# Rotary embedding of the attention queries and keys taken from PSUM by the vector engine, in place of a permutation matmul

## The reference, cut to what matters

```python
def rms_norm(x, g):
    y = xf * lax.rsqrt(jnp.mean(xf * xf, axis=-1, keepdims=True) + EPS)
    return y * g
def rope(x, pos):                      # hd = 128
    ang = pos[:, None] * inv[None, :]
    cos, sin = jnp.cos(ang), jnp.sin(ang)
    x1, x2 = xf[..., :hd // 2], xf[..., hd // 2:]
    return concatenate([x1 * cos - x2 * sin, x2 * cos + x1 * sin], axis=-1)

mq = rope(rms_norm(split_heads(mq, 8), moba_q_norm_g), pos)
mk = rope(rms_norm(split_heads(mk, 8), moba_k_norm_g), pos)
```

## Time and profile before

| | |
|---|---|
| Median of 3 runs | 1398.55 us |
| The profiled execution's own time | 1399.14 us |
| Its span | 1397.3 us |
| TensorE matmul busy | 1188.5 us (85%) |
| VectorE busy | 840.2 us (60%) |
| ScalarE busy | 466.0 us (33%) |
| GpSimd busy | 533.9 us (38%) |
| Mean granted TensorE clock | 0.955 |

### The profile page before, as it was taken

The page is one execution under the profiler, slowest core; times in us unless marked ns, Lnnn a source line. Parts: engine busy times, 40 slices in busy tenths (PEclk is TensorE's granted clock), DMA queues, the critical chain, the costliest instruction groups (busy, mean ns, idle before and its releaser), DMA issues.

```text
span 1397.3 us, 18240 instructions
## 1 busy us (share of the span) xinstructions
PE 1188.5 (85%) x5979; PEld 841.3 (60%) x5979; DVE 840.2 (60%) x1705; ACT 466.0 (33%) x866; POOL 533.9 (38%) x404
## 2 busy tenths in 40 slices
PE   6898898898899999789968978878787897978777
PEld 5798788788788999689544433434343353433232
DVE  4755746745755455556249666566665666666553
ACT  4544443443443455553023212222212222212211
POOL 3556456545546000000043544344344454454430
PEclk9999999999999999899989999999899899999999
DMA  6433333333232444348259999999999999999993
GB/s 201 113 84 102 90 90 93 87 93 102 75 106 78 120 121 120 90 137 277 83 217 412 419 416 421 415 421 419 418 421 415 422 421 422 422 421 422 421 421 135
DMA packets 182713, 355.02 MB, mean 254 GB/s; under 512 B 7959, under 2 KB 147598, under 8 KB 149774
## 3 DMA queue, kind: packets, MB, share of 16 engines
q0 software_dynamic: 36864, 268.45, 46.3%
q1 hardware_dynamic: 145806, 86.07, 21.4%
HBM read 353.45 MB, written 1.05 MB: 254 GB/s over the span
## 4 chain that ended last, share of the span: by engine, by line
PE 39%; DMA 32%; DVE 15%; ACT 7%; issue 6%; POOL 1%; SPq 0%; ACTq 0%; DVEq 0%; POOLq 0%
DMA top<-peer_uv_dram,route 17%; DMA scratch<-peer_uv_dram,route 10%; PE ps L1551 9%; PE ps L1271 6%; PE ps L1272 6%; PE ps L1273 6%; DMA front<-peer_uv_dram,route 4%; PE ps L1517 3%; DVE scratch L932 2%; PE ps L1386 2%; DVE scratch L937 2%; PE ps L1501 2%; PE ps L1405 2%; DVE scratch L934 1%; PE ps L1404 1%
## 5 line engine op out<-in xcount | busy, mean ns | idle before, releaser
L1271 PE MATMUL ps<-split 128*128 128x256 f32 (+1 forms) x960 | 289.2, 301 | 3.2 <-DVE split L896 3.2
L1272 PE MATMUL ps<-split 128*128 128x256 f32 (+1 forms) x960 | 269.9, 281 | 0.0
L1273 PE MATMUL ps<-split 128*128 128x256 f32 (+1 forms) x960 | 269.8, 281 | 0.0
L791 POOL TENSOR_TENSOR split<-front,split 128x1024 fp32r<-128x1024 f32 x80 | 192.1, 2411 | 195.7 <-ACT split L517 195.7
L1551 PE MATMUL ps<-top 128*128 128x512 f32 x448 | 214.6, 634 | 51.4 <-ACT top L747 51.4
L820 POOL DMA_INDIRECT front<-peer_uv_dram,route x80 | 87.6, 1095 | 374.3 <-DVE route L1133 250.7
L1551 PE MATMUL ps<-front,top 128*128 128x512 f32 x320 | 162.7, 661 | 46.5 <-ACT top L747 46.4
L1551 PEld LDWEIGHTS ps<-top 128*128 128x128 f32 x448 | 88.7, 203 | 169.3 <-issue 101.5
L1271 PEld LDWEIGHTS ps<-split 128*128 128x128 f32 x960 | 184.5, 192 | 8.0 <-DVE split L896 4.8
L820 POOL DMA_INDIRECT top<-peer_uv_dram,route x112 | 129.0, 1152 | 152.3 <-PE ps L1551 127.9
L1272 PEld LDWEIGHTS ps<-split 128*128 128x128 f32 x960 | 184.5, 192 | 3.2 <-issue 2.9
(11 more groups left out here) (240 smaller groups left out, 1784.6 us busy)
## 6 DMA issues: line engine op xcount, KB each, us to landing
front<-in_w_in_dram SPq DMA_DIRECT2D x88, 512.0 KB, 3.8
front<-in_w_branch_dram SPq DMA_DIRECT2D x24, 512.0 KB, 4.7
front<-in_w_mem_kv_dram SPq DMA_DIRECT2D x16, 512.0 KB, 3.9
front<-in_peer_w_q_dram SPq DMA_DIRECT2D x8, 1024.0 KB, 25.6
top<-in_w_out_dram SPq DMA_DIRECT2D x8, 512.0 KB, 6.1
top<-peer_uv_dram,route POOLq DMA_INDIRECT x112, 26.6
cst<-constants_dram SPq DMA_DIRECT2D x1, 1352.5 KB, 8.4
front<-peer_uv_dram,route POOLq DMA_INDIRECT x80, 25.9
```

What stands on the lines that cost most here:

```text
L791: pool.tensor_tensor(halves[i % 3][:, 1], raw[i % 3], halves[i % 3][:, 0], ALU.subtract).then_inc(lo_ready, 1)
L1271: pe.matmul(dst, lhs[0], rhs[0], start=first, stop=False)
L1272: pe.matmul(dst, lhs[0], rhs[1], start=False, stop=False)
L1273: return pe.matmul(dst, lhs[1], rhs[0], start=False, stop=last)
```

## The change

Both gains are multiplied into the rotation tables once, so that the table of q and the table of k are kept apart: `cos` and `sin` grow from 256 to 512 columns, and `swap` (128 columns) is dropped from the constants. The two scaled copies of ScalarE and the permutation matmul go. VectorE waits for the squares instead, multiplies bank 0 by `cos` (512 columns, 128 partitions), and makes the sine part in two instructions on 64 partitions each, which read the upper half of bank 0 and write the lower half of `rp2`, and the other way round. The event `rope_sin` now also guards bank 0: TensorE waits for it ahead of tile 4 (and ahead of the first memory tile). For head 0 it is counted once the tables are scaled. TensorE's wait for `dn_kept` moves from the dropped matmul to the next one that writes bank 4.

```diff
-    swap = np.zeros((P, P), np.float32)
...
-    cos, sin = np.concatenate([cos, cos]), np.concatenate([sin, sin])
+    cos, sin = np.concatenate([cos, cos]), np.concatenate([sin, -sin])
...
-        "cos": cos, "sin": sin, "levels": ...
+        "cos": np.concatenate([cos, cos], 1), "sin": np.concatenate([sin, sin], 1), "levels": ...
...
+        ev("rope_sin", 1)
+        rope_tables = sem("rope_tables")
...
                 act.activation(sqm, ps[:, 0, :], ACT.Square).then_inc(names["att_sq"].sem, 1)
-                act.activation(qg[:, 0:T], ps[:, 0, 0:T], ACT.Copy, scale=cols[:, R_MQ:R_MQ + 1])
-                act.activation(qg[:, T:HT], ps[:, 0, T:HT], ACT.Copy, scale=cols[:, R_MK:R_MK + 1]).then_inc(names["att_gain"].sem, 1)
...
             dve.tensor_tensor(memhT[:, 1], memraw, memhT[:, 0], ALU.subtract).then_inc(s_hlo, 1)
 
+            for table in (cos, sin):
+                for i, gain in enumerate((R_MQ, R_MK)):
+                    part = table[:, i * T:(i + 1) * T]
+                    dve.tensor_scalar(part, part, cols[:, gain:gain + 1], None, ALU.mult).then_inc(rope_tables, 1)
+            dve.wait_ge(rope_tables, 4)
+            dve.sem_inc(done("rope_sin"), 1)
...
-                on(dve, "att_gain", h)
-                dve.tensor_tensor(both(qk), both(qg), cos[:, None, :].to_broadcast([P, 2, T]), ALU.mult).then_inc(done("rope_cos"), 1)
-                on(dve, "att_rot", h)
-                dve.tensor_tensor(both(rp2), both(ps[:, 4, :]), sin[:, None, :].to_broadcast([P, 2, T]), ALU.mult).then_inc(done("rope_sin"), 1)
+                half = HD // 2
+                on(dve, "att_sq", h)
+                dve.tensor_tensor(qk, ps[:, 0, :], cos, ALU.mult).then_inc(done("rope_cos"), 1)
+                dve.tensor_tensor(rp2[0:half, :], ps[half:HD, 0, :], sin[half:HD, :], ALU.mult)
+                dve.tensor_tensor(rp2[half:HD, :], ps[0:half, 0, :], sin[0:half, :], ALU.mult).then_inc(done("rope_sin"), 1)
+                on(dve, "rope_cos", h)
                 on(dve, "rope_sin", h)
                 dve.tensor_tensor(qk, qk, rp2, ALU.add).then_inc(done("rope_sum"), 1)
...
+                on_before(pe, "rope_sin", h)
                 yield from tile("head", h, 4, ps[:, 0, 0:T], hT)
...
             def mem_tiles(it):
+                on_before(pe, "rope_sin", HEADS)
...
                 pe.matmul(ps[:, 3, :], ones, sqm, start=True, stop=True).then_inc(done("att_ss"), 1)
-                on_before(pe, "dn_kept", h)
-                on(pe, "att_gain", h)
-                pe.matmul(ps[:, 4, :], swap, qg, start=True, stop=True).then_inc(done("att_rot"), 1)
...
                 on(pe, "dn_kq", h)
+                on_before(pe, "dn_kept", h)
                 pe.matmul(ps[:, 4, :], kq[:, 0:P], kq, start=True, stop=True).then_inc(done("kq_dots0"), 1)
```

More of the change, by code:

```diff
@@ L105, in constants @@
     parts = {
-        "ident": ident, "after": after, "ones": ones, "swap": swap,
+        "ident": ident, "after": after, "ones": ones,
         "upto": np.concatenate([upto, ones, upto], 1),
         "mask": np.concatenate([causal, zeros, causal], 1),
-        "cos": cos, "sin": sin, "levels": np.concatenate(levels, 1), "eps": eps, "iota": iota,
+        "cos": np.concatenate([cos, cos], 1), "sin": np.concatenate([sin, sin], 1), "levels": np.concatenate(levels, 1), "eps": eps, "iota": iota,
     }
@@ L169, in const @@
             return cst[:, a:a + n]
-        ident, after, ones, swap = const("ident"), const("after"), const("ones"), const("swap")
+        ident, after, ones = const("ident"), const("after"), const("ones")
         upto, mask, cos, sin = const("upto"), const("mask"), const("cos"), const("sin")
@@ L228, in hybrid_layer @@
         HT = 2 * T
-        qg = carve(HT)
         sqm = carve(HT)
@@ L382, in on_before @@
             eng.wait_ge(e.sem, e.before(it))
-        for n in ("att_sq", "att_gain", "att_ss", "att_rot", "att_std", "rope_cos", "rope_sin", "rope_sum",
+        for n in ("att_sq", "att_gain", "att_ss", "att_std", "rope_cos", "rope_sum",
                   "att_rstd", "att_qk", "scores", "masked", "maxes", "negmax", "probs", "psums", "z_silu", "dn_scaled", "br_sum", "br_mix", "sig", "x1_ready", "x1_done", "gdots",
@@ L922, in head @@
                 b0, b1 = (small[:, bass.ds(h + (136 + 8 * c), 1)] for c in range(NC))
-                both = lambda a: a.rearrange("p (i t) -> p i t", i=2)
-                on(dve, "att_gain", h)
-                dve.tensor_tensor(both(qk), both(qg), cos[:, None, :].to_broadcast([P, 2, T]), ALU.mult).then_inc(done("rope_cos"), 1)
-                on(dve, "att_rot", h)
-                dve.tensor_tensor(both(rp2), both(ps[:, 4, :]), sin[:, None, :].to_broadcast([P, 2, T]), ALU.mult).then_inc(done("rope_sin"), 1)
+                half = HD // 2
[4 more added lines that the diff above has]
+                on(dve, "rope_cos", h)
                 on(dve, "rope_sin", h)
@@ L1016, in mem_head @@
                 on(dve, "att_rstd", it)
-                on(dve, "att_gain", it)
+                on(dve, "att_gain", it - HEADS)
                 dve.tensor_tensor(mqk4, mqk4, two(mstd)[:, :, None, :].to_broadcast([P, 2, 2, T]), ALU.mult).then_inc(done("att_qk"), 1)
@@ L1455, in mem_head @@
                 on(pe, "att_qk", it)
-                on(pe, "att_gain", it)
+                on(pe, "att_gain", it - HEADS)
                 for c in range(NC):
```

## The result

The changed kernel takes 1406.06 us (median of 5 runs, 1405.7 to 1408.32) against 1398.55 before (5 runs by then, with the same median): the ratio is 1.0056, with a 95% interval of 1.0041 to 1.007. It is slower by 7.5 us, where I had forecast 1399.2 and no measurable difference. The profiled execution took 1408.32 us (span 1406.5).

What follows compares the result with a forecast made beforehand. Last stage bound mostly by transfers; each head's start runs through ScalarE alone. Terms -5.8 + 0.6 + 4.05 + 1.8 = +0.65 us on the profiled 1399.14 gave 1399.8, so a median of 1399.2; range 1394.5 to 1403.0.

Steps and rivals of the forecast that it cites:

- ScalarE's chain, -5.8 us: Head loop: dropping two copies ahead of the table load saves 0.72 us a head, eight times.
- From L597 on, all engines hang on one another in the same order as before and move together: Head loop behind the square root: all engines and loads shift together, so the 0.72 us a head is kept.
- TensorE has room, 1.0 us: Head loop: without the permutation, TensorE's wait for the square root grows from 0.87 to 1.0 us; it doesn't become the bound.
- The tables: Prologue: four table multiplications on VectorE delay tile 4 by 4.7 us and the next link, `high(8)`, by 4.05 us.
- The clock behind the gap, +1.8 us: Prologue: after TensorE's idle gap, 4.3 us of tile 4 run at 1.2 GHz, 0.21 instead of 0.12 a matmul.
- More constants, +0.6 us: Start of the kernel: 192 KB more constants delay the small rows the first matmul waits for, and so everything.
- The prologue's terms: Start and prologue: constants +0.6, tables +4.05 and slower clock +1.8 us.
- Rival 3: Head loop: crosswise reads between partitions are slow, sum ends 2.3 us past the root, eight times: 1418 us; chance 0.05.
- Rivals 1 and 2: Prologue: gap only 2.6 us, clock holds, 1395.3, chance 0.17; gap as forecast but clock holds, 1397.4, chance 0.14.
- Rival 4: Head loop: another wait holds ScalarE, so dropping the copies wins nothing: 1405 us; chance 0.06.

Runs made afterwards that it cites:

- Experiment 5: Changed kernel with table scaling moved 20 us earlier, plus three unread TensorE products in its two longest waits of a head: 1394.39 us, ratio 0.9969.
- experiment 7: Kernel before plus only four VectorE multiplications by 1.0 in the prologue, TensorE waiting for them ahead of tile 4: 1406.57 us, ratio 1.0058.
- experiment 10: Changed kernel plus five unread 512-column TensorE products during its wait for the tables ahead of tile 4 of head 0: 1404.23 us, ratio 1.004.
- Experiment 6: Kernel before plus one more unread 256-column ScalarE copy per head, making heads longer: 1402.38 us, ratio 1.0023.
- experiment 8: Changed kernel with table scaling moved earlier, plus each head's two square roots and their reciprocals kept in PSUM: 1367.28 us, ratio 0.9774.

## Why the prediction was wrong

- **ScalarE's chain, -5.8 us: the step that failed.** The saving per head up to the root was right (6.40 us from the squares to it before, 5.67 after: 0.73). The step that failed is "From L597 on, all engines hang on one another in the same order as before and move together". TensorE does not move with them when its clock falls. The seven distances gained 4.2 us (0.37, then 6 x 0.64) and lost 5.2 in four falls (1.1 and 3 x 1.4); with head 7 the whole loop came out 0.3 longer instead of 5.8 shorter. I had counted a falling clock for the prologue's gap alone and never asked it of waits that were already there and stayed as long as before. Experiment 5 brings 5.7 us back by filling them; its loop is 4.8 shorter than before, so even without falls 1.0 of the 5.8 is missing: 0.64 a head, not 0.72, and less in head 0.
- **TensorE has room, 1.0 us: right.** L1355 waits 0.99. So does VectorE: 2.93 us idle ahead of the reciprocal, forecast 3.0.
- **The tables: right.** 2.48, 2.43 and two undisturbed ones were forecast, a start of tile 4 at 47.2 and a gap of 4.7; measured are 2.46, 2.42 and twice 0.34, a start at 47.20 and a gap of 4.37. That start is better than the method deserves: between profiles the stage ahead of the tables moved by up to 1.5 us (41.38 in experiment 7, 42.83 in experiment 10).
- **The clock behind the gap, +1.8 us: too small.** The slow level lasted 6.1 us of the two tiles instead of 4.3, and cost 2.6. In experiment 7 it lasted 3.3 behind nearly the same gap: the forecast took one gap's figure for a fixed one.
- **More constants, +0.6 us: not seen at the start.** The first matmul began at 11.16 in the changed kernel and at 11.20 before, and no run tests the term by itself.
- The prologue's terms, constants included, came to 6.45; it cost 6.7 (4.1 for the wait, 2.6 for the clock). That they agree so well is luck: the clock's 0.8 too little and the constants' 0.6 too much cancel. Of the error of the whole, 6.9 us, the loop has 6.1.
- Rival 3, the crosswise reads, fell with the 0.69 us rows. Rivals 1 and 2 fell with the 4.37 us gap and the 0.21 pace. Rival 4 named the right outcome, a loop that wins nothing, and a sum of 1405, for a wrong reason: no other wait holds L562.

Against the kernel before on the same chip, the medians go from 7.5 us above to 1.9 above with the tables early, and to 3.8 below with the waits filled: 5.6 us for the prologue and 5.7 for the loop's clock. The forecast for the last state was 5.8 less 0.6 for the constants, 5.2 below.

Why falls are so much more frequent with heads of 50.5 us is not settled. The two waits are there in the kernel before, 1.16 and 1.90 us long, and bring nothing in its eight heads, nor in the two profiles with 51.2. Heads with a fall and heads without one have the same two waits, to 0.02 us. That the moment matters at which a head meets the clock's control is likely, but I have only argued it. Experiment 6 was meant to show it; its single fall in eight heads neither shows nor excludes it.

## What to carry to other kernels

A shorter chain is worth its length only while TensorE's clock holds. Look for pairs of waits of one or two microseconds close together, even old ones: here products that nobody read, put into them, brought 5.7 us back. A profile without a fall doesn't prove that the next execution has none. A wait of some 4 us put ahead of dense matmuls in a prologue cost itself and a slow stretch behind it here; small preparations belong where their engine is idle and GpSimd isn't running. When an elementwise operation is several times longer than its like of the same shape, see what GpSimd runs beside it. If it reads two operands from SBUF, try one of them in PSUM.

## What the runs showed of the hardware

- VectorE reading PSUM on partitions 64 to 127 and writing SBUF on 0 to 63 costs 0.69 us for 512 columns, as an operation on all 128 partitions without the shift.
- A VectorE multiplication of 128x512 with two SBUF operands took 2.51 us when GpSimd's subtraction had begun 0.43 us ahead, and 0.69 when the multiplication began first, by 0.16 us. With one operand in PSUM it took 0.69 beside the same subtraction (155.61 to 158.01 and 156.05 to 156.74 in head 2 of experiment 8). 3.4 us of each head was this wait, 27 us in all. The Trainium skill, SBUF — State Buffer, section "Who interferes with whom", says that a VectorE instruction with two SBUF inputs reads the second through an interface shared with GpSimd, that the first to issue holds the shared pair for its whole instruction, and that one with at most one SBUF input, outside the modes that use both ports, stays out of it; these runs agree. One SBUF input was not enough by itself: the four multiplications of 128x256 by a constant in experiment 7 (SBUF to SBUF) took 5.21 us together, two of them beside the subtractions, where one alone takes 0.34.
- Reciprocals and roots with operand and result in PSUM cost what they cost in SBUF (reciprocal 3.37 against 3.35 us, root 0.66 against 0.69).
